# A decoder layer on one core: who issues the sample's attention loads, and in which order the output projection begins

## The reference

```
xn   = RMSNorm(x);  q, k, v = split(proj(xn))           # 8 heads of 64
for window, dilation in (128,1), (512,4), (2048,16):    # keys gathered by stride
    s = q k^T / 8, masked to the band;  m = max(s);  p = exp(s - m)
    o_c = p v;  l_c = sum(p);  lse_c = m + log(l_c)
y_att = sum_c softmax_c(lse_c) * o_c / l_c              # three dilations merged
h  = x + concat(y_rwkv, y_att) @ w_out                  # 1024 x 1024
hn = RMSNorm(h);  route hn to experts;  h += experts(hn);  y = RMSNorm(h)
```

## Time and profile before

| what | us |
|---|---|
| median of three runs (3611.78 to 3618.81) | 3616.51 |
| the profiled execution's own time | 3613.6 |
| its span, first to last instruction | 3611.8 |
| attention, barrier to barrier (about 1610 to 2150) | 540 |
| output projection up to its first product (2150.3 to 2201.2) | 50.9 |

### The profile page before, as it was taken

The page is one execution under the profiler, slowest core; times in us unless marked ns, Lnnn a source line. Parts: engine busy times, 40 slices in busy tenths (PEclk is TensorE's granted clock), DMA queues, the critical chain, the costliest instruction groups (busy, mean ns, idle before and its releaser), DMA issues. The chain is left out here.

```text
span 3611.8 us, 75172 instructions
## 1 busy us (share of the span) xinstructions
PE 3211.5 (89%) x31053; PEld 2206.1 (61%) x31054; DVE 1320.0 (37%) x3264; ACT 1005.5 (28%) x2145; POOL 324.3 (9%) x344
## 2 busy tenths in 40 slices
PE   6999999999879888969898976996799999999990
PEld 4667766667668888857666663554455555555550
DVE  3445434444134433326444425664311111111117
ACT  3334443333222222326333343331011111111112
POOL 0000000000011000104223000000011001110114
PEclk9999999999689999989988858998899999999995
DMA  6121111111543223337545435430677877677757
GB/s 210 50 70 65 60 54 60 49 56 56 66 169 112 111 99 112 126 103 261 176 122 150 101 119 175 153 122 21 238 255 260 288 244 244 233 258 250 247 194 292
DMA packets 298182, 544.44 MB, mean 151 GB/s; under 512 B 98322, under 2 KB 122642, under 8 KB 291268
## 3 DMA queue, kind: packets, MB, share of 16 engines
q1 hardware_dynamic: 262980, 441.86, 37.2%
q0 software_dynamic: 20784, 73.15, 5.5%
q10 hardware_dynamic: 14160, 25.70, 2.1%
HBM read 400.66 MB, written 139.98 MB: 150 GB/s over the span
## 5 line engine op out<-in xcount | busy, mean ns | idle before, releaser
L294 PE MATMUL proj_main_ps<-proj_xt,proj_w 128*128 128x257 f32 (+1 forms) x1728 | 390.7, 382 | 0.0
L294 PEld LDWEIGHTS proj_main_ps<-proj_xt,proj_w 128*128 128x128 f32 x1728 | 328.8, 204 | 40.9
L2407 PE MATMUL moe_gate<-moe_w,moe_xt 128*64 128x256 f32 x2624 | 299.2, 381 | 6.6 <-DMA moe_w<-in_expert_w_dram 5.9
L2423 PE MATMUL moe_y_ps<-moe_w,moe_ht 128*64 128x512 f32 x1312 | 301.0, 601 | 3.1 <-ACT moe_ht L2462 3.1
L2407 PE MATMUL moe_up<-moe_w,moe_xt 128*64 128x256 f32 x2624 | 301.3, 383 | 0.0
L2407 PEld LDWEIGHTS moe_gate<-moe_w,moe_xt 128*64 128x64 f32 x2624 | 189.4, 138 | 136.7 <-issue 47.3
L317 PE MATMUL proj_main_ps<-proj_w,proj_xt 128*128 128x512 f32 (+1 forms) x560 | 248.0, 597 | 0.0
L2160 PE MATMUL out_proj_ps<-out_w,out_ct 128*128 128x512 f32 x544 | 240.0, 595 | 0.0
L2407 PEld LDWEIGHTS moe_up<-moe_w,moe_xt 128*64 128x64 f32 x2624 | 180.4, 137 | 97.4 <-issue 13.6
L1609 DVE CUSTOM_DVE_ANT_0 att_sc<-att_s_ps,att_mask 128x256 f32<-128x256 f32 (+1 forms) x384 | 117.4, 361 | 189.7 <-PE att_s_ps L1455 123.0
L2423 PEld LDWEIGHTS moe_y_ps<-moe_w,moe_ht 128*64 128x64 f32 x1312 | 87.3, 137 | 158.4 <-issue 155.0
(11 more groups left out here) (334 smaller groups left out, 5146.3 us busy)
## 6 DMA issues: line engine op xcount, KB each, us to landing
moe_w<-in_expert_w_dram SPq DMA_DIRECT2D x96, 2048.0 KB, 10.1
y_rows<-rwkv_zero POOLq DMA_DIRECT2D x65, 512.0 KB, 4.8
y_rows<-moe_y ACTq DMA_DIRECT2D x164, 128.0 KB, 6.1
ft_p<-proj_uf SPq DMA_DIRECT2D x32, 642.0 KB, 3.3
rwkv_feat<-ft_p SPq DMA_DIRECT2D x16, 1284.0 KB, 7.0
att_s_k<-in_cache_att_k_dram SPq DMA_DIRECT2D x16, 1024.0 KB, 9.6
att_s_v<-in_cache_att_v_dram SPq DMA_DIRECT2D x16, 1024.0 KB
o_p<-att_o SPq DMA_DIRECT2D x48, 260.0 KB, 2.1
```

The source lines that it names most:

```text
L294: last = mm(out[:, 0:w + 1], W[:, k, kind * C + m * P:kind * C + (m + 1) * P], XT[n % 2][:, k, 0:w + 1], start=(k == 0), stop=(k == KT - 1))
L2407: last = mm(bank[j * HB:(j + 1) * HB, 0:HF], XT[:, q, r * HB:(r + 1) * HB], W[:, k, j * HF:(j + 1) * HF], start=(k == 0), stop=(k == KT - ...
L2423: last = mm(py[j * HB:(j + 1) * HB, :], HT[:, c, r * HB:(r + 1) * HB], W2[s][:, k, j * 512:(j + 1) * 512], start=(k == 0), stop=(k == FE / ...
```

## The change

In attention `NM` becomes one buffer with a place for each of the 48 blocks, and DVE no longer waits for stores. The sample's loads for sequences 1 to 7 (56 transfers) move from SP to ACT: at the end of iteration u, after ACT's copies, ACT issues at most one large load, at fixed distances from at(b). The loads of sequence 0 stay on SP, and the sample's stores move one block later. In the output projection SP loads the identity right behind tile 0, spreads gates and x between the tiles, and puts the gain and router constants late; ACT issues `W` in two halves, after tile 0 has landed. DVE starts on tile 0 when that tile is there, prepares tile 0, then runs `unit_rows(1)` and the first gate before the rest of tile 1. PE turns tile 1 between the two products of tile 0. The constants are waited for where they are used.

```diff
-        NM = ring("nm", [P, H], NO)
+        NM = sb("nm", [P, NBK, H])
...
-                sp.dma_start(dst(m_out), NM[n % NO][:]).then_inc(o_st[n % NO], 16)
+                sp.dma_start(dst(m_out), NM[:, n, :]).then_inc(o_st[n % NO], 16)
...
-                    if n == (at(b) - 7) // 2 and b + 1 < B:
-                        if b >= 1:
-                            sp.wait_ge(s_prod, 3 * b)
-                        load_sample_q(b + 1)
-                        load_sample_k(b + 1, 0)
-                        load_sample_k(b + 1, 1)
-                    if n == (at(b) - 3) // 2 and b + 1 < B:
-                        load_sample_k(b + 1, 2)
-                    if n == (at(b) + 9) // 2:
-                        if b + 1 < B:
-                            load_sample_v(b + 1)
+                    if n == (at(b) + 11) // 2:
                         store_sample(b)
...
+            def load_sample_v(b, g):
+                if b >= 1:
+                    a.wait_ge(s_weighted, b)
+                cached(SV, cache_v, b, g, sv_ld)
+                if g == 2:
+                    a.dma_start(VN[:], qkv_s[b * T:(b + 1) * T, 2 * C:3 * C]).then_inc(sv_ld, 16)
+
+            def sample_loads(u):
+                for b in range(B + 1):
+                    if b >= 2:
+                        for g in range(3):
+                            if u == at(b) - (9, 8, 7)[g]:
+                                load_sample_v(b - 1, g)
+                    if b + 1 < B:
+                        if u == at(b) - 6:
+                            load_sample_k(b + 1, 0)
+                        if u == at(b) - 5:
+                            load_sample_q(b + 1)
+                        if u == at(b) - 4:
+                            load_sample_k(b + 1, 1)
+                        if u == at(b) - 2:
+                            load_sample_k(b + 1, 2)
...
                 for b in range(B):
                     if u == at(b):
                         sample_exp(b)
+                sample_loads(u)
...
-                if n >= NO and half == 0:
-                    v.wait_ge(o_st[n % NO], 32 * (n // NO))
...
             load(0)
+            sp.dma_start(cn[:], consts).then_inc(ident_in, 16)
+            load_gates(0)
             load(1)
-            sp.dma_start(cn[:], consts).then_inc(c_in, 16)
-            load_gates(0)
             load_gates(1)
+            load_x(0)
             load(2)
             load_gates(2)
+            load_x(1)
             sp.dma_start(gf[:], row(g_ffn, D)).then_inc(c_in, 16)
...
-            for t in range(NB):
-                load_x(t)
+            load_x(2)
...
-            v.wait_ge(c_in, 16 * 6)
-            for t in range(2):
-                unit_rows(t)
-                merge_weights(t)
-                merge(t)
+            unit_rows(0)
+            merge_weights(0)
+            merge(0)
+            unit_rows(1)
             gate(0)
+            merge_weights(1)
+            merge(1)
...
-            nc.scalar.dma_start(W[:], w_out.rearrange("(k p) n -> p k n", p=P)).then_inc(w_in, 16)
+            a.wait_ge(ld[0], loaded(0))
+            for j in range(2):
+                cols = slice(512 * j, 512 * (j + 1))
+                nc.scalar.dma_start(W[:, :, cols], w_out.rearrange("(k p) n -> p k n", p=P)[:, :, cols]).then_inc(w_in[j], 16)
...
-            pe.wait_ge(c_in, 16 * 6)
+            pe.wait_ge(ident_in, 16)
             turn_cat(0)
-            pe.wait_ge(w_in, 16)
             for t in range(NT):
-                if t + 1 < NT:
+                if 1 <= t and t + 1 < NT:
                     turn_cat(t + 1)
...
+                if t == 0:
+                    pe.wait_ge(w_in[0], 16)
                 product(t, 0).then_inc(low, 1)
+                if t == 0:
+                    turn_cat(1)
+                    pe.wait_ge(w_in[1], 16)
```

More of the change, by code:

```diff
@@ L1556, in exps @@
                     a.wait_ge(masked, 4 * u + hl + 1)
-                    nc.scalar.activation(SC[u % NSC][:, hl, k0:], SC[u % NSC][:, hl, k0:], ACT.Exp, bias=NM[n % NO][:, 4 * half + hl:4 * half + hl + 1], scale=-1.0).then_inc(exped, 1)
+                    nc.scalar.activation(SC[u % NSC][:, hl, k0:], SC[u % NSC][:, hl, k0:], ACT.Exp, bias=NM[:, n, 4 * half + hl:4 * half + hl + 1], scale=-1.0).then_inc(exped, 1)
             def p_copy(u):
@@ L1571, in o_copy, with load_sample_q, cached, load_sample_k @@
                 nc.scalar.copy(O[n % NO][:, 4 * half:4 * half + 4, :].rearrange("p h k -> p (h k)"), o_ps[u % 2][:, 0:4 * VW]).then_inc(o_copied, 1)
+            def load_sample_q(b):
+                if b >= 2:
+                    a.wait_ge(s_prod, 3 * (b - 1))
+                rows = qkv_s[b * T:(b + 1) * T, 0:C]
+                a.dma_start(SQ[b % 2][:], rows.rearrange("(o t) k -> o t k", o=1).broadcast_to([P, T, C])).then_inc(sq_ld[b % 2], 16)
+            def cached(dst, src, b, g, loaded):
+                one = src[b]
+                rows = (one[N - P:N, :].rearrange("(i d) k -> i d k", d=1), one[N - 4 * P:N, :].rearrange("(i d) k -> i d k", d=4),
+                        one[N - 16 * P:N, :].rearrange("(i d) k -> i d k", d=16)[:, 0:T, :])[g]
+                a.dma_start(dst[:, key_group(g), :], rows).then_inc(loaded, 16)
+            def load_sample_k(b, g):
+                if b >= 1:
+                    a.wait_ge(s_prod, 3 * (b - 1) + g + 1)
+                cached(SK, cache_k, b, g, sk_ld[g])
+            def load_sample_v(b, g):
+                if b >= 1:
+                    a.wait_ge(s_weighted, b)
+                cached(SV, cache_v, b, g, sv_ld)
+                if g == 2:
+                    a.dma_start(VN[:], qkv_s[b * T:(b + 1) * T, 2 * C:3 * C]).then_inc(sv_ld, 16)
+            def sample_loads(u):
+                for b in range(B + 1):
+                    if b >= 2:
+                        for g in range(3):
+                            if u == at(b) - (9, 8, 7)[g]:
[9 more added lines that the diff above has]
+                            load_sample_k(b + 1, 2)
             def sample_exp(b):
@@ L1768, in output_projection @@
         lg_ps = ps("lg_ps")
-        c_in, w_in = sem("consts_loaded"), sem("w_loaded")
+        ident_in, c_in, w_in = sem("ident_loaded"), sem("consts_loaded"), [sem(f"w_loaded{j}") for j in range(2)]
         ld = [sem(f"loaded{j}") for j in range(NB)]
@@ L2113, in hn_copy @@
                 last.then_inc(hn_copied, 1)
[L2115 to L2119 removed]
+            a.wait_ge(ld[0], loaded(0))
+            for j in range(2):
+                cols = slice(512 * j, 512 * (j + 1))
+                nc.scalar.dma_start(W[:, :, cols], w_out.rearrange("(k p) n -> p k n", p=P)[:, :, cols]).then_inc(w_in[j], 16)
+            y_squares(0)
+            merge_exp(0)
+            y_root(0)
+            y_squares(1)
             cat_copy(0)
+            merge_exp(1)
+            y_root(1)
             for t in range(NT + 1):
```

22 lines of the change are left out of this document (10 added, 12 removed).

## The result

The changed kernel takes 3498.14 us, median of four runs (3485.69 to 3517.56), against 3617.66 us for the kernel before in the same session (3611.78 to 3636.33, four runs): a ratio of 0.9666, 95% interval 0.9609 to 0.9723. The forecast was 3519, with a range from 3487 to 3563. The profiled execution is the slowest of the four: 3517.56 us, with a span of 3515.8.

What follows compares the result with a forecast made beforehand. Attention was held by DVE's store wait, PE's lower clock and otherwise PE's work, the projection's start by transfers and a constants wait. 3613.6 - 72 (46 + 30 - 4) - 25 = 3516.6, median 3519; own range 3500 to 3540, 8-in-10 range 3487 to 3563.

Steps and rivals of the forecast that it cites:

- PE's idle time in attention: Attention: without DVE's wait for the maxima's stores, PE's three idle rows go, 46.4 us gained.
- ACT asks for the same stores, next to nothing left: Attention: ACT needs the stores three iterations later, 7.8 us at the least, so next to no wait remains.
- The clock: Attention: with the gaps gone PE runs less at 1.2 GHz, 30 us gained, bounds nothing to 38 us.
- The last stretch at the full clock: Attention's last 54 us, at 0.50 before, run at full clock once DVE's last wait goes: 15 us gained.
- rival 1: Attention: the clock isn't tied to gaps and falls as often; gain 67 us, time 3549; chance 0.20.
- ACT's issues: Attention: ACT's 56 added transfers mostly fit beneath its wait for PE; 4 us charged, bounds 0 to 197 us.
- Rival 4: Attention: slow issues hold ACT and the exponentials PE needs; at the longest 96 us slower, 3712; chance 0.04.
- Rival 2: Attention: stores land late and the wait moves to ACT; gain 47 + 25 us, time 3545; chance 0.07.
- stores no longer stand behind large loads: Attention: with the sample's loads on ACT, the store of maxima lands in a few microseconds; the sum doesn't rest on it.
- The smaller signs: Attention profile: PE idle under 10 us, granted clock near 0.95, ACT's wait for PE's output from 100 to some 70 us.
- The projection: Output projection: DVE starts at T + 6, first product T + 20.5, tile 1's T + 40.5 to 42; 25 us gained.
- Rival 3: Output projection: little earlier, PE waiting at W's second half or tile 2; gain 72 + 10 us, 3534; chance 0.13.

Runs made afterwards that it cites:

- run 4: The changed kernel again, nothing altered, on the chip of a later session: 3478.81 us, ratio 0.9710 to the kernel before.
- run 10: The changed kernel again, nothing altered, on another chip: 3487.51 us, ratio 0.9739 to the kernel before.
- run 1: The kernel before with only a place in NM for each block and no DVE wait for stores: 3513.51 us, ratio 0.9809.
- run 2: The kernel before with only the sample's loads on ACT and its stores one block later; DVE's wait stays: 3551.50 us, ratio 0.9906.
- run 5: The changed kernel with the sample's loads left on SP and its stores in their old place: 3487.85 us, ratio 0.9668 to the kernel before.
- run 6: The changed kernel with one more tiny load issued by ACT in each of 96 iterations: 3486.36 us, ratio 0.9656 to the kernel before.
- run 12: The changed kernel with DVE's wait for five router and norm constants put back before its first projection row: 3501.53 us, one execution.
- run 3: The kernel before with only the new output projection, attention as before: 3548.75 us, ratio 0.9907.
- Run 9: The changed kernel with W loaded by ACT during the last iterations of attention: 3484.46 us, ratio 0.9721 to the kernel before.
- run 11: The changed kernel with W as one 4 MB load instead of two halves, behind tile 0's rows: 3485.65 us, one execution.

## Why the prediction was right

The time fell in the range, and the two places where time is gained are as told, and in both the wait that was named is the cause. It isn't the whole of the prediction that held: the sum met the profiled execution partly by errors that cancelled (clock 26.5 for 30, ACT 0 for 4, projection 26.7 for 25, a first unit 4.0 us later for nothing). The median, 3498, lies 2 us under the forecast's own range of 3500 to 3540, and also under what the best cases named in the prediction add up to: 46 of idle time, 38 of clock, 31 of projection and nothing for ACT make 115 us, or 3502. Only the 15 us below that, down to 3487, which the prediction puts down to stalls that it hadn't priced, cover it. In the other two sessions the change gave 104 us (run 4) and 89 us (run 10), on either side of the forecast's 97. By the steps:

- **PE's idle time in attention:** forecast 46.4 us, measured 46.7. That it comes from the one wait is shown by run 1.
- **ACT asks for the same stores, next to nothing left:** right; no such wait in any profile.
- **The clock:** forecast 30 us with an upper bound of 38. This is the term that was mis-sized. The kernel before lost 50.4 us to it, not 38. By an estimate some 3 us of that lie in the first 18 us of the stage (granted clock 0.69 from 1622 to 1640), which my window from 1640 on left out. I also took 0.32, the loss of 128-key units, for all work: in four iterations of longer units the same 131 matmuls took 27.4 us at a mean clock of 0.55 in run 2 (from 1840.4) and 17.9 us at 1.00 in run 5 (from 1840.8), which makes a loss of some 0.39 at 0.50, an estimate. The rest I can't place. The gain was 26.5 us in the first profile and 44 in run 4. Averaged over the three profiles with waits (50, 57, 28) and the ten without (23.9, 6.5, 23.8, 0, 2.1, 28.3, 0.7, 22.8, 0.7, -1.5; mean 10.7) it is about 34.
- **The last stretch at the full clock** (15 of these 30 us): wrong in the profiled execution, where rival 1 had it right. The fall doesn't need a gap. In the ten profiles without DVE's wait and with the old order of blocks the last stretch was at 0.50 four times and at 1.00 six times, the same kernel both ways (changed and runs 10 and 4). Each time it fell where the last sample's weighing, 20 matmuls of 512 columns, had just ended. The prediction named "a clock that falls without a wait will still fall" but priced it at nothing there, and named a last stretch at 0.50 as a sign of being wrong: by that sign this step failed.
- **Why the median lies 21 us under the forecast:** the profiled execution, 3517.56 us, met the forecast with its last stretch at 0.50 (mean clock 0.942). The other three have mean clocks of 0.950 to 0.955 and take 3486 to 3498 us. A last stretch at 1.00 is worth about 23 us by the table (above 421.0, the four profiles with 0.50 have 24.7 in the mean and the six with 1.00 have 1.4). That this is what set them apart is not shown, since only one of them was profiled, and the late start of the attention in the profiled execution (up to 20 us) is another candidate.
- **ACT's issues:** forecast 4 us of cost; none can be told (runs 5 and 6). The sum charged ACT for the whole of each issue, and no run shows that ACT computes nothing meanwhile; in the trace the issue lies beneath the running copy. The cover was larger than I took, for the wait ahead of the output copy isn't the only one that gives way, and 0.33 us replaces SP's 0.52. Rival 4's slow issues didn't appear: ACT's longest key load took 0.43 us.
- **Rival 2:** refuted. Stores land up to 13.3 us late and no engine waits. The sentence that stores no longer stand behind large loads bought nothing: the median landing is 3.6 us, where the kernel before had 2.6.
- **The smaller signs:** PE idles for 10.1 us (forecast under 10), the granted clock is 0.91 (near 0.95), and ACT's wait for PE's output is 88.2 us (some 70). All three point the right way and fall short.
- **The projection:** forecast 25 us, measured 26.7. DVE at T + 6.7 (forecast 6), first product T + 21.7 (20.5), tile 1's T + 40.1 (40.5 to 42), last constant T + 32.7 by run 12 (34 to 36). So the times are nearly right, the way to them isn't. I had the first product wait for tile 1's landing at T + 17 to T + 18 and then the gate. DVE took up tile 1 at T + 14.2 without a wait and ended the gate at T + 17.8, and PE then waited 5.37 us for W: its first half landed at T + 21.6, not T + 14, as its 2 MB took 14.9 us beside SP's queue, about 140 GB/s and not 259. And tile 1's product followed at once on tile 0's second half, without the wait for DVE that I had put there. The pieces of that step, 20.5 + 7 + 2 + 1 + 7, also make T + 37.5, not the 38.5 of the prediction.
- **Rival 3:** refuted; W's second half cost PE 0.6 us.

## What to carry to other kernels

When a ring of small buffers holds up an engine behind a store, look first at giving each item its own place: here 4 KB stores beside megabytes of loads landed up to 12.9 to 13.8 us late with SP issuing the loads (runs 1, 3 and 5) and up to 9.6 to 13.3 with ACT (run 2 and the changed kernel), and moving the loads alone left 38 us of waiting, while a place for each item left none. Hold back an engine's first instruction for nothing but what that instruction reads; one wait for constants, which DVE first reads 36 us after its first instruction in the changed kernel, was 23 of 26 us here. And split a stage's time into PE's idle and PE's busy time at an equal count of matmuls: the difference of the busy times is then what the clock costs, with no need to work from a rounded mean clock.

## What the runs showed of the hardware

- A granted clock of 0.50 came with PE busy for 70.00 of 70 us, and of 72 us for 71.24, and ahead of both falls it was busy for 39.90 of 39.90 us at 1.00. The Trainium skill, "TensorE: Matmul & The Clock Gate", Part 1, says that the throttled state is the default and that activity releases it; by that alone these stretches should have been at 2.4 GHz, and the measurement decides. The same kernel ran the same stretch at 1.00 in another execution. Most of the falls at a busy PE began right behind a sample's weighing (1796 in runs 5 and 6, 1784 in run 4, about 2004 in the changed kernel and run 6); shorter ones began elsewhere (about 1782 in the changed kernel, 1762 in run 10). Why only behind some weighings stays open. It wasn't tried whether breaking these matmuls up prevents it.
- Run 9's six runs fall in two groups: 3465 to 3473 us at mean clocks of 0.953 to 0.955, and 3496 to 3501 us at 0.943 to 0.944. A median of a few runs can hit either.
- An issue of a transfer on ACT started 0.01 us after ACT's copy had begun and lasted 0.33 us beside it (1739.27). With 96 issues more, 25.2 us of "issue" stood ahead of ACT's exponentials, and the time didn't grow (run 6).
- W's 4 MB landed in 16.2 us as one load at the start of the stage, in 20.5 us as one load behind tile 0's rows (run 11), and in 25.1 us for the later of two halves issued there.
